# Modulation weights split over the layer: eight blocks first, forty as pairs of column tiles between other stages, and rope inside the projection

## The chip, the cores and the metric

The kernel runs on one core of a Trainium2 chip. The metric is the device time of one execution in microseconds (us), the median over several executions. The engines are named as in the profile: PE is TensorE (PEld its weight loads), DVE VectorE, ACT ScalarE, POOL GpSimd, SP SyncE, which here only issues the weight transfers. A name with q behind it is an engine's queue of instructions.

## The reference

Two layers work on 6 tiles of 128 tokens (4 latent, 2 context) with 1024 channels. What matters here, shortened:

```python
mod = silu(c) @ w_mod[l] + b_mod[l]        # (6 * 1024), one row for the latents, one for the context
sh1, sc1, g1, sh2, sc2, g2 = split(mod, 6)
h = layer_norm(x) * (1 + sc1) + sh1
p = h @ w_in[l]                            # 22 blocks of columns: conv, A, B, D, O
yA = windowed_gqa(rope(qA), rope(kA), vA)  # A: 4 + 2 tiles of 128 channels turned by rope
yB, yC, yD = neighbourhood(...), conv_module(...), mlstm(...)
y = merge(yA, yB, yC, yD, gates(h)) @ w_out[l]
x = layer_norm(alpha * x + g1 * y)         # deepnorm, first sub-layer
h2 = layer_norm(x) * (1 + sc2) + sh2
x = layer_norm(alpha * x + g2 * experts(h2, router(h2)))   # 16 experts, each takes its own tokens
```

w_mod of a layer is 1024 x 6144, i.e. 24 blocks of 256 columns (1 MB each). The shift and scale vectors are needed with channels on partitions (`modc`), the gates g1 and g2 as rows.

## The kernel before

All work goes through 27 stages. At the end of each, the four engines PE, ACT, DVE and POOL meet: `Stages.leave` (L472) drains the engine, adds one to a semaphore and waits until all four have done so. A drain on POOL also waits for the transfers that POOL issued. The stages of layer 0 are: modulation, modulate (transpose the normalised tiles, scale and shift), in-projection of the conv, A and B blocks, rope, attention, in-projection of the D blocks, mLSTM, O projection, merge, out-projection, router, gather, experts, closing norm. The closing norm of layer 0 shares its time with layer 1's modulation. Layer 1 has the same stages, shorter ones since it needs no context output.

SP runs ahead of the stages. It loads 1 MB blocks of weights into a ring of four slots (`raw`, `load`), in one fixed order: 24 of w_mod, 22 of w_in, 24 of gate and branch, 4 of w_out, then the experts'. A slot is free when PE has used it (`ring_used`) or, for the w_in and gate blocks, when its remainder is split off. Of those blocks ACT copies the high part (L457) and POOL or DVE computes the low part (L460) into `part`, two blocks deep. For the conv, A and B blocks DVE does that between the taps of the depthwise convolution (31 taps over 4 tiles, given out evenly between blocks); for the others, and for the first two blocks of a stage, POOL does it. PE takes a block only when its remainder is there.

The modulation stage: PE multiplies the 1024 x 2 columns `s2T` with each block into two PSUM rows; DVE adds the bias over two blocks at a time (L1445) into `mod_row`; 32 small transposes (L762) and four DVE instructions (L1451) make `modc`; POOL stores `mod_row` to `mod_d` in DRAM (L577), from which the gate rows are read later (L635).

```python
for c in range(MOD_BLOCKS):                          # PE, L753
    w = take()
    passes(psf[0:2, ...], [(s2T[:, k, :], w[:, k, :]) for k in range(KD)]).then_inc(ring_used, 1)
```

Rope is a stage of its own behind the in-projection: six matmuls (L815) with a rotation matrix, three DVE instructions each. Behind POOL's last remainder of the in-projection POOL stores the convolution's input to the attention, `yc_d` (L592). In the out-projection PE waits for the router's weights before the first tile, though it needs them from the third on. At the start of the experts DVE sets three buffers to zero (L1919), POOL one (L656), and then DVE computes the first two remainders (L1868).

## Time and profile before

| | us |
|---|---|
| median of 3 runs | 4023.34 |
| lowest, highest | 4022.8, 4026.16 |
| the profiled execution | 4029.46 |
| its span in the trace | 4027.8 |
| TensorE busy | 3587.6 (89%) |
| VectorE busy | 2335.1 (58%) |
| ScalarE busy | 1588.6 (39%) |
| GpSimd busy | 741.7 (18%) |

The span is the time from the first to the last instruction of the profiled execution. Busy shares are averages over stages that differ much, so that they say little of any one stage. The stages' ends in the trace are the moments at which the engines leave a meeting; for layer 0: 107.9, 138.0, 391.0, 404.9, 597.8, 716.9, 787.9, 834.4, 1270.1, 1398.2, 1431.8, 1471.2, 2179.3 and 2283.8.

### The profile page before, as it was taken

Reading aid. Unit: us, or ns where it says so; the run is one execution under the profiler, and the core shown is the slowest. Engines: PE = TensorE matmul, PEld = TensorE weight load, DVE = VectorE, ACT = ScalarE, POOL = GpSimd, SP = SyncE. Lnnn points to the kernel's source line nnn. Section 1 sums busy time; section 2 is a strip of 40 time slices with the busy share of each in tenths; the row PEclk is TensorE's granted clock in tenths of the full one; section 3 lists DMA queues with packets and bytes.
Section 4 is the critical chain, followed back from the end, with each engine's and each line's share of the span. In section 5 each row is a group of like instructions: output and inputs, shape, how many; then the busy total and the mean of one; then the engine's idle time right before and its main releaser. Section 6 shows DMA issues by size and latency. Waiting matters only on the chain. (4 is left out here: it accounts for less than half of the span.)

```text
span 4027.8 us, 49164 instructions
## 1 busy us (share of the span) xinstructions
PE 3587.6 (89%) x18834; PEld 2743.3 (68%) x18834; DVE 2335.1 (58%) x3474; ACT 1588.6 (39%) x2055; POOL 741.7 (18%) x403
## 2 busy tenths in 40 slices
PE   8797889899998869999998699798899868999994
PEld 3697569888887756666664388578766655666663
DVE  2295761511111659999897464751322258999996
ACT  0321762511110236666662222553311126666662
POOL 0100012111110013332231100011222103233221
PEclk9899999899999889999998799899999979999997
DMA  9121022011112228888887621131122217999994
GB/s 317 61 73 69 21 79 71 12 68 56 40 63 74 94 82 306 311 309 311 308 307 273 206 79 63 43 100 53 37 94 94 84 64 270 327 325 334 331 324 152
DMA packets 329455, 632.73 MB, mean 157 GB/s; under 512 B 12288, under 2 KB 102480, under 8 KB 322880
## 3 DMA queue, kind: packets, MB, share of 16 engines
q1 hardware_dynamic: 309056, 557.88, 40.0%
q0 software_dynamic: 20240, 72.64, 5.3%
q8 instruction: 111, 1.82, 0.2%
q14 instruction: 48, 0.39, 0.0%
HBM read 613.95 MB, written 16.52 MB: 157 GB/s over the span
## 5 line engine op out<-in xcount | busy, mean ns | idle before, releaser
L733 PE MATMUL ps<-hx,part 128*128 128x384 f32 (+2 forms) x4704 | 928.9, 357 | 32.2 <-DVEq L474 17.3
L733 PEld LDWEIGHTS ps<-hx,part 128*128 128x128 f32 x4704 | 834.4, 190 | 115.7 <-DVEq L474 18.5
L1094 PE MATMUL ps<-part,hx 128*96 128x512 f32 x3072 | 759.0, 397 | 38.3 <-DVE part L1868 31.1
L1094 PEld LDWEIGHTS ps<-part,hx 128*96 128x96 f32 x3072 | 492.7, 163 | 249.1 <-DVE part L1868 49.7
L1868 DVE TENSOR_TENSOR part<-raw,part 128x2048 fp32r<-128x2048 f32 x256 | 615.4, 2404 | 26.1 <-ACT part L1356 24.3
L1356 ACT ACTIVATE part<-raw 128x2048 fp32r<-128x2048 f32 x256 | 489.9, 1914 | 214.0 <-PE ps L1094 188.9
L460 POOL TENSOR_TENSOR part<-raw,part 128x2048 fp32r<-128x2048 f32 x52 | 237.6, 4570 | 1165.9 <-ACT part L457 1165.9
L1094 PE MATMUL ps<-hx 128*96 128x512 f32 x1536 | 378.9, 395 | 4.0 <-DVE hx L1868 2.4
L1094 PEld LDWEIGHTS ps<-hx 128*96 128x96 f32 x1536 | 247.3, 162 | 112.9 <-POOL hx L680 5.7
L733 PE MATMUL ps<-part,hx 128*128 128x256 f32 (+2 forms) x2208 | 307.5, 301 | 15.5 <-DVEq L474 15.5
L733 PEld LDWEIGHTS ps<-part,hx 128*128 128x128 f32 x2208 | 289.0, 194 | 30.9 <-DVEq L474 16.2
L1761 DVE TENSOR_TENSOR area<-ps,area 128x768 f32<-128x768 f32 (+1 forms) x48 | 39.6, 825 | 425.6 <-PE ps L733 425.6
L733 PE MATMUL ps<-area,raw 128*128 128x384 f32 (+1 forms) x768 | 285.3, 521 | 0.0
L1875 DVE TENSOR_TENSOR area<-area,ps 128x512 f32<-128x512 f32 x340 | 225.6, 679 | 73.2 <-PE ps L733 73.2
L1868 DVE TENSOR_TENSOR hx<-raw,hx 128x2048 fp32r<-128x2048 f32 x96 | 233.8, 2436 | 49.2 <-ACT hx L1356 49.2
L1356 ACT ACTIVATE hx<-raw 128x2048 fp32r<-128x2048 f32 x128 | 244.5, 1910 | 43.1 <-PE ps L1094 32.3
L733 PE MATMUL ps<-hx 96*128 96x512 f32 x680 | 214.1, 414 | 47.0 <-DVE hx L1913 38.9
L733 PEld LDWEIGHTS ps<-area,raw 128*128 128x128 f32 x768 | 145.0, 190 | 107.9 <-issue 46.0
L680 POOL TENSOR_TENSOR hx<-raw,hx 128x2048 fp32r<-128x2048 f32 x32 | 148.1, 4628 | 350.0 <-ACT hx L1356 350.0
L1489 DVE SCALAR_TENSOR_TENSOR area<-area,conv_c 128x512 f32<-128x512 f32 x360 | 208.8, 659 | 0.0
L733 PEld LDWEIGHTS ps<-hx 96*128 96x128 f32 x680 | 126.0, 194 | 106.2 <-issue 49.4
L733 PE MATMUL ps<-raw,s2T 128*2 128x256 f32 x768 | 174.6, 391 | 24.5 <-DVE area L1445 10.0
(244 smaller groups left out, 3807.8 us busy)
## 6 DMA issues: line engine op xcount, KB each, us to landing
raw<-in_w_exp_gate SPq DMA_DIRECT2D x128, 1024.0 KB, 5.3
raw<-in_w_exp_up SPq DMA_DIRECT2D x128, 1024.0 KB, 5.3
raw<-in_w_exp_down SPq DMA_DIRECT2D x128, 1024.0 KB, 5.4
raw<-in_w_mod SPq DMA_DIRECT2D x48, 1024.0 KB, 6.4
raw<-in_w_in SPq DMA_DIRECT2D x44, 1024.0 KB, 4.8
raw<-in_w_gate SPq DMA_DIRECT2D x32, 1024.0 KB, 5.4
area<-in_bias POOLq DMA_DIRECT2D x32, 512.0 KB, 4.0
raw<-in_w_branch SPq DMA_DIRECT2D x16, 1024.0 KB, 8.6
```

The source lines that it names most:

```text
L460: self.tt.tensor_tensor(part[:, q % 2, 1, :], raw[:, n % RING, :], part[:, q % 2, 0, :].bitcast(f32), ALU.subtract).then_inc(S("split_p"), 1)
L680: nc.gpsimd.tensor_tensor(expert_part(s, 1), raw[:, (r0 + s) % RING, :].rearrange("p (k n) -> p k n", k=4), expert_part(s, 0).bitcast(f32) ...
L733: last = mm(dst, a, b, start=i == 0, stop=i == len(pairs) - 1)
L1094: last = mm(ps[0:CAP, bank, :], x, y, start=kh == 0 and a == 0, stop=kh == 1 and a == len(pairs) - 1)
L1356: fn(expert_part(s, 0), src, ACT.Copy).then_inc(S("split_h"), 1)
L1489: own(V.scalar_tensor_tensor(y, x, conv_c[:, j, tap:tap + 1], y, ALU.mult, ALU.add))
L1761: V.tensor_tensor(even(t_) if ctx_out else t_[:, 0:LAT], p_, s_, ALU.mult).then_inc(*S("z_part", l).by(1))
L1868: V.tensor_tensor(expert_part(s, 1), src, expert_part(s, 0).bitcast(f32), ALU.subtract).then_inc(S("split_v"), 1)
L1875: V.tensor_tensor(a, a, ps[:, scatter_bank(c, ncomb), :], ALU.add).then_inc(*S("e_acc", l).by(1))
```

## The change

Only the eight blocks with sh1 and sc1 of layer 0 stay in front. The other 40 (16 of layer 0, 24 of layer 1) are taken in 20 pairs by `mod_pair(g, i)` of PE. A pair computes 4 x 128 columns as four column tiles, one in each quarter of the PSUM partitions (rows 0, 32, 64, 96), one k at a time through all four. `MOD_GROUPS` gives the six groups of pairs and their places, all in layer 0: two pairs between the transposes of modulate (group 0), four ahead of A and B blocks (1), four ahead of D blocks (2), one between the halves of the O projection and one at its end (3), eight in the router stage (4 and 5), of which two stand ahead of the wait for the affinities and six ahead of the slots' transposes. DVE's `move_mod(g)` adds the bias in four instructions of two partitions; POOL's `load_mod_bias(g)` and `store_mod(g)` issue four small transfers for each run of pairs of one layer. `modc` of sh2 and sc2, and all four of layer 1, are read back from `mod_d` by POOL's `load_modc`, eight numbers for each partition, each number apart. SP follows `PLAN`.

Further parts: rope's matmuls stand inside the A and B blocks (`ROPE_AT`), with one PSUM bank and one temporary; DVE does the turns of the first three between remainders and of the others at the end; the copies out of PSUM have three groups of banks instead of four (D blocks: two instead of three); the taps are given out over 7 blocks instead of 8; one meeting is gone from each layer. POOL's store of `yc_d` stands ahead of its last two remainders. ACT's first two high parts of layer 0 stand behind tiles 3 and 4 of modulate, and in the O projection both next ones at the end. PE waits for `router_in` at the third tile. DVE's first two expert remainders stand ahead of the zeroing, and POOL's zeroing in the router stage.

TensorE from the program's start: the modulation and modulate stages, and the start of the in-projection. Before:

```order
L733 MATMUL ps<-raw,s2T 2x256 x192
L762 MATMUL ps<-consts,area 128x2 x32
L771 MATMUL ps<-consts,area 128x128 x48
L733 MATMUL ps<-hx,part 128x512 x24
L733 MATMUL ps<-hx,part 128x256 x24
```

Now:

```order
L835 MATMUL ps<-raw,s2T 2x256 x64
L875 MATMUL ps<-consts,area 128x2 x16
L884 MATMUL ps<-consts,area 128x128 x8
L862 MATMUL ps<-raw,s2T 2x128 x32
L884 MATMUL ps<-consts,area 128x128 x8
L862 MATMUL ps<-raw,s2T 2x128 x32
L884 MATMUL ps<-consts,area 128x128 x32
L835 MATMUL ps<-hx,part 128x512 x24
```

A block in front is 8 matmuls of 256 columns; 64 of 192 are left, and each `L862 ... x32` is one pair.

TensorE in the A and B blocks of the in-projection of layer 0 and behind them. Before (the last row is rope):

```order
L733 MATMUL ps<-hx,part 128x384 x288
L733 MATMUL ps<-part,hx 128x144 x144
L733 MATMUL ps<-hx,part 128x384 x384
L733 MATMUL ps<-part,hx 128x256 x288
L815 MATMUL ps<-area 128x512 x6
```

Now, from the second block on (L931 is rope):

```order
L862 MATMUL ps<-raw,s2T 2x128 x32
L835 MATMUL ps<-part,hx 128x144 x144
L931 MATMUL ps<-area 128x512
L862 MATMUL ps<-raw,s2T 2x128 x32
L835 MATMUL ps<-hx,part 128x384 x144
L931 MATMUL ps<-area 128x512
L835 MATMUL ps<-hx,part 128x384 x96
L931 MATMUL ps<-area 128x512
L835 MATMUL ps<-hx,part 128x384 x96
L931 MATMUL ps<-area 128x512
L835 MATMUL ps<-hx,part 128x384 x48
L835 MATMUL ps<-part,hx 128x256 x120
```

Two of the four pairs and four of the six rope matmuls are seen; each stands in the one queue of TensorE ahead of the rest of the projection.

GpSimd from the D blocks of layer 0 (stores of attention's buffers) to the end of the O projection. Before:

```order
L612 DMA area<-yc_d 128x3072
L613 DMA ya_d<-area 128x3072
L460 TENSOR_TENSOR part<-raw,part 128x2048 x6
L622 TENSOR_TENSOR area<-area 128x512 x12
L460 TENSOR_TENSOR part<-raw,part 128x2048 x2
L629 DMA area<-ya_d 128x3072
```

Now:

```order
L697 DMA area<-yc_d 128x3072
L698 DMA ya_d<-area 128x3072
L620 DMA area<-in_b_mod 2x2x128 x8
L512 TENSOR_TENSOR part<-raw,part 128x2048 x6
L638 DMA modc<-mod_d 128x8x1 x4
L643 TENSOR_SCALAR modc<-modc 128x16
L628 DMA mod_d<-area 2x2x128 x8
L713 TENSOR_TENSOR area<-area 128x512 x12
L620 DMA area<-in_b_mod 2x2x128 x4
L512 TENSOR_TENSOR part<-raw,part 128x2048 x2
L628 DMA mod_d<-area 2x2x128 x4
L724 DMA area<-ya_d 128x3072
```

The bias loads stand ahead of the six remainders, the `modc` loads and eight stores behind them; the same kind of stores stands behind the remainders of the O projection.

The diff, cut to its core:

```diff
+MOD_FIRST = 8
+MOD_GROUPS = (((0, 4), (0, 5)), ((0, 6), (0, 7), (0, 8), (0, 9)), ((0, 10), (0, 11), (1, 0), (1, 1)),
+              ((1, 2), (1, 3)), ((1, 4), (1, 5), (1, 6), (1, 7)), ((1, 8), (1, 9), (1, 10), (1, 11)))
+MOD_BANKS = (4, 7, 4, 4, 7, 5)
+ROPE_AT = (12, 15, 17, 19, 25, 28)
+MOD_AB, MOD_D, MOD_O = (5, 6, 7, 8), (15, 16, 17, 18), (21,)
...
@@ GpSimd
-                for p in range(2, MOD_BLOCKS // BIAS):
-                    pool.wait_ge(*S("mod_row", l).at((p - 1) * BIAS // 2))
-                    load_mod_bias(p)
-                pool.wait_ge(*S("mod_row", l).at(MOD_BLOCKS // 2))
-                load(mod_d[l], mod_row[0:2, :]).then_inc(*S("mod_out", l).by(16))
-                pool.wait_ge(*S("mod_out", l).at(16))
+                def store_mod(g):
+                    pool.wait_ge(*S("mod_moved", 0).at(g + 1))
+                    for layer, p, i, n in mod_runs(g):
+                        dst = mod_d[layer, :, 4 * P * p:4 * P * (p + n)].rearrange("s (q c n) -> c s q n", q=n, c=4)
+                        for c in range(4):
+                            load(dst[c], mod_tiles(g)[32 * c:32 * c + 2, 0, i * P:(i + n) * P].rearrange("s (q n) -> s q n", q=n)
+                                 ).then_inc(*S("mod_stored", 0).by(16))
+                def load_modc(layer, vs):
+                    for v in vs:
+                        row = (0, 1, 3, 4)[v]
+                        for s in range(2):
+                            load(modc[:, v, :, s], mod_d[layer, s, row * D:(row + 1) * D].rearrange("(k p) -> p k", p=P),
+                                 allow_slow_non_contiguous=True).then_inc(*S("modc_in", l).by(16))
+                    pool.wait_ge(*S("modc_in", l).at(32 * len(vs)))
...
                 split.mixers_to(l, 2)
+                if l == 0:
+                    load_mod_bias(0)
+                    store_mod(0)
+                    load_mod_bias(1)
+                    stored(0)
                 st.leave()
...
                 pool.wait_ge(*S("conv_tapped", l).at(1))
+                load(yc_d[:, :, 0:full * P], yc[:, :, 0:full * P]).then_inc(*S("yc_out", l).by(16))
                 split.mixers_from(l, S_D)
                 split.mixers_to(l, S_D + 2)
-                load(yc_d[:, :, 0:full * P], yc[:, :, 0:full * P]).then_inc(*S("yc_out", l).by(16))
-                st.leave()
...
                 split.mixers_to(l, S_O + 2)
+                if l == 0:
+                    load_modc(0, (2, 3))
+                    store_mod(2)
+                    stored(2)
...
@@ TensorE
+                def mod_pair(g, i):
+
+                    if g and i == 0:
+                        pe.wait_ge(*S("mod_moved", 0).at(min(g, 4)))
+                    ws = [take(), take()]
                     for k in range(KD):
+                        for c in range(4):
+                            last = mm(ps[32 * c:32 * c + 2, MOD_BANKS[g], i * P:(i + 1) * P], s2T[:, k, :],
+                                      ws[c // 2][:, k, c % 2 * P:(c % 2 + 1) * P], start=k == 0, stop=k == KD - 1)
+                            if k == KD - 1 and c % 2:
+                                last.then_inc(ring_used, 1)
...
+                def rope(j):
+                    if j == 0:
+                        pe.wait_ge(*S("rope_in", l).at(32))
+                        pe.wait_ge(*S("ab_out", l).at(6))
+                    if j >= 1:
+                        pe.wait_ge(*S("rope_done", l).at(j))
                     src = y_v[0][:, j, 0:LAT] if j < FB else kA[:, j - FB, 0:LAT]
-                    mm(ps[:, j % 2, :], rot, src, start=True, stop=True).then_inc(*S("rope_rot", l).by(1))
+                    mm(ps[:, 6, :], rot, src, start=True, stop=True).then_inc(*S("rope_rot", l).by(1))
...
-                pe.wait_ge(*S("router_in", l).at(16))
                 for t in range(full + 2):
...
+                        if t == 2:
+                            pe.wait_ge(*S("router_in", l).at(16))
...
+                if l == 0:
+                    mod_pair(4, 0)
+                    mod_pair(4, 1)
                 pe.wait_ge(*S("r_aff", l).at(1))
...
@@ VectorE
-                share = -(-len(taps) // (S_D - S_AB - 2))
-                for q in range(S_AB + 2, S_D):
+                share = -(-len(taps) // (S_D - S_AB - 3))
+                for q in range(S_AB + 2, S_D - 1):
                     convolve(share)
                     split.mixers_to(l, q + 1)
+                    if q == S_AB + 6:
+                        if l == 0:
+                            move_mod(1)
+                        dve.wait_ge(*S("rope_in", l).at(32))
+                    if q >= S_AB + 6:
+                        rope(q - S_AB - 6)
...
+                for s in range(AHEAD):
+                    if not rest_rank(s)[0]:
+                        rest(0, s)
                 for v, cols in ((put, TOK), (y_hi, D), (y_lo, D)):
```

## Rows read from the trace of the kernel before

**Rows 1.** The page's part 4: the chain that ended last, by engine.
```profile
PE 25%; DVE 4%; issue 4%; ACT 2%; DMA 1%; POOL 1%; POOLq 0%; DVEq 0%; ACTq 0%; SPq 0%
```

**Rows 2.** Windows, one for each of these stages; the header names the columns.
```profile
core 0: us, PE busy (x) PEld busy (x) DVE busy (x) ACT busy (x) POOL busy (x), PEclk, DMA share, GB/s
0.00:107.90 107.90, 89.10 (x416) 35.19 (x416) 23.68 (x52) 4.00 (x9) 9.31 (x21) 0.97 0.93 308
107.90:138.00 30.10, 11.00 (x48) 9.00 (x48) 11.40 (x6) 26.91 (x56) 11.86 (x3) 0.56 0.20 70
138.00:391.00 253.00, 236.20 (x1488) 227.79 (x1488) 160.71 (x268) 48.16 (x61) 10.76 (x5) 0.97 0.19 67
...
597.80:716.90 119.10, 111.69 (x704) 107.24 (x704) 14.77 (x29) 33.82 (x40) 28.63 (x8) 0.98 0.22 71
...
787.90:834.40 46.50, 39.09 (x312) 38.42 (x312) 12.31 (x24) 9.49 (x15) 9.10 (x2) 0.94 0.07 24
...
1398.20:1431.80 33.60, 2.26 (x12) 1.38 (x12) 28.17 (x59) 1.57 (x2) 1.00 (x2) 0.50 0.02 3
1431.80:1471.20 39.40, 38.50 (x160) 31.40 (x160) 0.00 (x0) 18.68 (x24) 0.00 (x0) 0.95 0.00 0
...
2179.30:2283.80 104.50, 90.27 (x416) 35.93 (x416) 67.92 (x112) 3.72 (x13) 7.49 (x14) 0.91 0.82 274
...
2526.60:2540.50 13.90, 8.46 (x12) 2.86 (x12) 11.43 (x18) 0.00 (x0) 0.00 (x0) 0.75 0.00 1
```

**Rows 3.** Timeline of VectorE: start, duration, engine, line, operation (idle before).
```profile
45.26 0.68 DVE L1445 TENSOR_TENSOR area<-ps,area 2x512 f32<-2x512 f32 x1 [6.23 <-PE ps L733]
```

**Rows 4.** Timeline of VectorE: layer 1's last standardise.
```profile
2245.34 0.81 DVE L1431 TENSOR_SCALAR area<-area,stat 128x1024 f32<-128x1024 f32 x1
```

**Rows 5.** Groups by form of the whole run: remainders on GpSimd, DMA issues.
```profile
L460 POOL TENSOR_TENSOR part<-raw,part 128x2048 fp32r<-128x2048 f32 x52 | 237.6, 4570 | 1165.9 <-ACT part L457 1165.9
...
L561 POOL DMA_DIRECT2D area<-in_b_mod x6 | 3.1, 519 | 52.9 <-DVE area L1445 46.4 <-DMA x_d<-area 6.5
```

**Rows 6.** Timeline, all engines, at the start of the out-projection, layer 0.
```profile
1268.07 0.37 SPq L510 DMA_DIRECT2D raw<-in_w_out  x1
...
1272.56 0.90 POOL L636 DMA_DIRECT2D area<-in_w_router  x1
...
1283.39 18.90 PE L733 MATMUL ps<-raw,area 128*128 128x256 f32 x73 [15.35 <-DMA area<-in_w_router]
```

**Rows 7.** DMA issues of the whole run: count, KB each, median us to landing.
```profile
raw<-in_w_mod SPq DMA_DIRECT2D x48, 1024.0 KB, 6.4
raw<-in_w_in SPq DMA_DIRECT2D x44, 1024.0 KB, 4.8
...
area<-in_w_router POOLq DMA_DIRECT2D x2, 64.0 KB, 9.7
```

**Rows 8.** The same place in layer 1, TensorE.
```profile
3185.76 17.46 PE L733 MATMUL ps<-raw,area 128*128 128x256 f32 x69 [12.83 <-DMA area<-in_w_router]
```

**Rows 9.** Groups by form of the whole run (busy us, mean ns): modulation matmuls.
```profile
L733 PE MATMUL ps<-raw,s2T 128*2 128x256 f32 x768 | 174.6, 391 | 24.5 <-DVE area L1445 10.0 <-ACT s2T L1125 8.8 <-DMA raw<-in_w_mod 4.7
```

**Rows 10.** Timeline of TensorE in the attention stage, layer 0.
```profile
439.01 1.14 PE L832 MATMUL ps<-area 128*64 128x128 f32 x16 [0.34 <-ACT area L1212]
```

**Rows 11.** Groups by form of the whole run: the rope's matmuls.
```profile
L815 PE MATMUL ps<-area 128*128 128x512 f32 x24 | 16.6, 824 | 35.7 <-ACTq L474 32.6 <-DVE area L1518 3.0
```

**Rows 12.** Timeline of VectorE in the in-projection, layer 0.
```profile
329.05 2.29 DVE L460 TENSOR_TENSOR part<-raw,part 128x2048 fp32r<-128x2048 f32 x1
331.25 14.24 DVE L1489 SCALAR_TENSOR_TENSOR area<-area,conv_c 128x256 f32<-128x256 f32 x27
```

**Rows 13.** Timeline of GpSimd at the end of the in-projection, layer 0.
```profile
380.99 0.56 POOL L592 DMA_DIRECT2D yc_d<-area  x1
```

**Rows 14.** Timeline of VectorE at the end of the router stage, layer 0.
```profile
1425.64 6.11 DVE L1849 TENSOR_TENSOR part<-iotas,area 128x512 fp32r<-128x512 f32 x10
```

**Rows 15.** Timeline of VectorE at the start of the experts, layer 0.
```profile
1471.22 9.09 DVE L1919 TENSOR_SCALAR hx<-consts 96x768 fp32r<-96x768 f32 x3 [39.47 <-ACTq L474]
```

**Rows 16.** Timeline of TensorE at the start of the experts, layer 0.
```profile
1483.55 4.69 PE L1094 MATMUL ps<-part,hx 128*96 128x512 f32 x12 [13.22 <-DVE part L1868]
```

More of the change, by code:

```diff
@@ L968, in _ @@
                 for half in range(2):
+                    if l == 0 and half:
+                        mod_pair(3, 0)
                     w = take_split()
@@ L1034, in _ @@
                 last.then_inc(*S("r_affT", l).by(1))
+                if l == 0:
+                    mod_pair(4, 2)
+                    mod_pair(4, 3)
+                    for i in range(4):
+                        mod_pair(5, i)
                 pe.wait_ge(*S("slots", l).at(1))
@@ L1174, in copies @@
                             between[g]()
-                        act.wait_ge(*pa.of(B_IN + b, j))
+                        if l == 0 and what == "vB" and idx == (0, 0):
+                            act.wait_ge(*S("mod_stored", 0).at(128))
+                        act.wait_ge(*pa.of(ORD[l]["in", b], j))
                         bank = 2 * (g % depth)
@@ L1292, in _ @@
                     fn(sig_o[:, g % 2, :], ps[:, g % 2, 0:QC], ACT.Sigmoid).then_inc(*S("o_sig", l).by(1))
-                    if t == full - 1:
+                    if t == full - 1 and (l or half):
                         split.mixers_to(l, S_O + half + 3)
@@ L1521, in _ @@
                     dve.wait_ge(*S("rope_done", l).at(j + 1))
-                    V.tensor_tensor(q, q, rope_s[:, j % 2, :], ALU.add)
+                    own(V.tensor_tensor(q, q, rope_s, ALU.add))
+                share = -(-len(taps) // (S_D - S_AB - 3))
+                for q in range(S_AB + 2, S_D - 1):
+                    convolve(share)
+                    split.mixers_to(l, q + 1)
+                    if q == S_AB + 6:
+                        if l == 0:
+                            move_mod(1)
+                        dve.wait_ge(*S("rope_in", l).at(32))
+                    if q >= S_AB + 6:
+                        rope(q - S_AB - 6)
+                assert not taps
+                own.wait()
+                dve.drain().then_inc(*S("conv_tapped", l).by(1))
+                split.mixers_to(l, S_D)
+                for j in range(S_D - S_AB - 7, 6):
+                    rope(j)
                 st.leave()
@@ L1926, in _ @@
                 dve.drain().then_inc(*S("e_yL", l).by(2))
-                for s in range(AHEAD):
-                    if not rest_rank(s)[0]:
-                        rest(0, s)
                 with turns(dve, E // 2 - 1) as i:
```

318 lines of the change are left out of this document (202 added, 116 removed).

## The prediction, made before the changed kernel ran

> **What bounds the kernel now.** I read the chain that ended last first. TensorE holds 25% of the span there, VectorE and issue 4% each, all other engines 2% or less [rows 1]: no single engine is the limit everywhere, and the rest of the span is many short hand-overs. So the change has to be priced stage by stage, and the second view is the windows [rows 2], cut where the four engines meet. In a window the reader is to see which engine is nearly full and whether DMA is. Four kinds appear:
> - 0.00 to 107.90 (modulation, layer 0) and 2179.30 to 2283.80 (closing norm of layer 0 with layer 1's modulation): DMA share 0.93 and 0.82 at 308 and 274 GB/s. Each is 24 blocks of 1 MB with two output rows, and weight delivery is the limit.
> - 138.00 to 391.00, 597.80 to 716.90, 787.90 to 834.40: TensorE busy 236 of 253, 112 of 119, 39 of 46.5, DMA share 0.07 to 0.22. There is room for weights, none for TensorE time.
> - 1398.20 to 1431.80 (router): VectorE busy 28 of 33.6, TensorE 2.3, DMA share 0.02.
> - 1431.80 to 1471.20 (gather): TensorE 38.5 of 39.4, DMA 0.00.
>
> The kernel before spends about 3.4 us per block (1.05 MB at 308 GB/s) on 48 modulation blocks with nothing beside them, while DMA idles elsewhere.
>
> **What the change removes**, in us.
> 1. Modulation stage of layer 0. Eight blocks stay. VectorE's fourth addition, which ends block 8, is at 45.26 and takes 0.68 [rows 3]; 16 transposes, two additions and the meeting add 2: the stage ends at 48.0 where it ended at 107.9. **-59.9**.
> 2. Layer 1's modulation. Its last block loads are gone; what is left is VectorE's last standardise at 2245.34 + 0.81 [rows 4]. Beside it GpSimd loads four parameters and then eight `modc` loads. VectorE is no longer last; GpSimd is. Layer 0's last stores, four issues (0.52 each [rows 5]) and their landing reach to about 2240, an estimate; eight issues of 0.90 (nearest row: `w_router`, also 1024 pieces, [rows 6]) give 2247, and 2.5 for landing 2249.5, where the stage ended at 2283.8. **-34.3**. Both ends for the landing: 0.5 and 9.7 [rows 7].
> 3. The rope as a stage of its own: 13.9 in layer 1 [rows 2] and the same in layer 0. See 5 and 10.
> 4. `router_in` waited on at the third tile only. TensorE idles 15.35 until 1283.39 for `w_router` [rows 6]. The last of four w_out blocks is issued at 1268.07; with 4.8 to land, as for w_in [rows 7], TensorE can start at 1272.9. **-10.5**. Layer 1: 12.83 of idle until 3185.76 [rows 8]; by the same landing **-8.0**. VectorE needs rows that GpSimd issues just ahead of `w_router`, but not before TensorE's first run, which is 18.90 long [rows 6], so they are there.
>
> **What it adds.** First a pair's price, which no row shows. One block now is 16 records in 174.6 / 48 = 3.64, so 0.227 a record of 256 columns [rows 9]; a record of 128 columns is half, 0.114. A pair is 64 such records. One after another: 7.3. Four at once: 1.8. The nearest row has two column tiles: 16 records in 1.14 [rows 10], 0.071 each where 0.114 would be serial, a gain of 1.6 from two tiles, so that tiles do overlap. I take **2.1**, near the lower end. The Trainium skill (TensorE: Matmul & The Clock Gate, section "Why this matters for your kernels") gives 2.38 for three column tiles; by that share a pair would be 2.3 and the sum 2 us more, an estimate.
>
> 5. In-projection of layer 0. Four pairs (+8.4), six rope matmuls on TensorE (0.824 each [rows 11], +4.9), and depth 3 instead of 4. VectorE must convolve 31 taps per block instead of 27, from 14.24 to 16.3, plus its 2.29 remainder [rows 12]: 18.6 a block, where TensorE needs 16.6, so that it eats its lead of about one block by block 13, and `rope(1)` waits some 6 for VectorE. I put the stalls at 15. `yc_d` was issued at 380.99 [rows 13], behind GpSimd's last remainder (4.6 [rows 5]) and ScalarE's part and copy (2.3), so TensorE ended at 374.1; now at 374.1 + 8.4 + 4.9 + 15 = 402.4, and the last remainder 6.9 later: 409.3. The store held the meeting until 391.0; it is now issued ahead of the last two remainders and is covered. With the rope the two stages ended at 391.0 + 13.9 = 404.9. **+4.4**. Both ends: no stall gives -10.6, twice the stall +19.4.
> 6. Stage 1 (modulate, 30.1 long, [rows 2]). ScalarE's first two parts move behind tiles 3 and 4, so GpSimd's remainders (4.57) end near 30 instead of running beside. Then, in one queue: four bias DMAs (2.1), landing 3 to 5, VectorE's move 1.7, four stores 2.1, landing 2, four more bias issues 2.1. **+13**, to 43. The pairs sit in TensorE's idle time (11 busy of 30).
> 7. D projection: four pairs, +8.4. Behind the last remainder GpSimd has four `modc` loads (3.6 issue, 3 landing), 1, and eight stores (4.2) that must land (2.5). **+22.7**. The eight bias loads ahead are hidden under TensorE.
> 8. O projection: one pair ahead (2.1), two remainders at the end instead of one (+4.6), four stores (2.1), landing 2.2. **+11**.
> 9. Router of layer 0: 16 blocks, four of them already in the ring. The first of the other twelve lands 6.4 [rows 7] after a slot is free at about 1.2, eleven more follow at 3.4: 45.0. Then the pair's end 0.9, slot transposes 0.8, a copy 0.3 and VectorE's 6.11 [rows 14]: 53.1 against 33.6. **+19.5**. The store and second move of groups 4 and 5 lie under the gather's 39.4 (VectorE and DMA empty there), as do the first expert loads.
> 10. Layer 1's in-projection and rope: as in 5 without pairs. The meeting at 2526.6 stood behind a smaller store, its last remainder some 9 earlier at 2517.6; 5.6 for the rope matmuls and their waits: 2523.2 against 2540.5. **-17.3**.
> 11. Start of the experts, both layers. TensorE starts at 1483.55, 12.35 after the barrier, after VectorE's zeroing of 9.09 [rows 15] and its first remainder [rows 16]. Now the remainders come first, so TensorE may start 8 earlier, but the third remainder waits for the zeroing: **-4.5** each, -9.
>
> Sum: -59.9 -34.3 -18.5 +4.4 +13 +22.7 +11 +19.5 -17.3 -9 = **-68.4**. The terms come from the profiled execution of 4029.46 (span 4027.8, 1.7 around it); it is 6.1 above the median of 4023.34. Nothing in the terms scales with that, so I subtract from the median: 4023.3 - 68.4 = **3955**.
>
> **Rivals.**
> - *The filled places are not that expensive (larger gain).* My stalls in 5 (15), the landing chains in 6 and 7 (about 10 together) are estimates that can be zero: -25, **3930**. For: DMA share is 0.2 there. Against: the `yc_d` row, where a store held a meeting 10 us. 0.12.
> - *VectorE becomes the bound of the in-projection.* With 18.6 per block against 16.6 the lead may be gone at once, and blocks behind a pair arrive late in the ring of four: 8 us for two loads, at eight places 2 to 4 each, beside 15 for VectorE. +20 to +40, **3985**. For: [rows 12]. Against: TensorE's own rate hides single loads. 0.14.
> - *The four tiles run one after another.* A pair costs 7.3: 12 pairs ahead of the router at +5.2, 62, and eight in it, where 7.3 against 6.8 of delivery adds 4: +66, **4021**, no change. For: the two-tile row gains 1.6 and not 2. Against: it gains. 0.06. That the tiles are thus not what the diff says is this case.
> - *Single-element loads* (the other side). `load_modc` reads 1024 numbers of 4 bytes per DMA. I priced its issue 0.90 as for 1024 longer pieces. If each instead costs the 9.7 that `w_router` took to land, one behind the other, 12 of them cost 12 x (9.7 - 0.9) = 106: **4061**, slower. It decides from 68 / 12 = 5.7 extra each. For: the row of 9.7 is the only such load. Against: beside it, megabyte loads competed for the queues. The Trainium skill (DMA: Bandwidth & Descriptors, section "Rules for kernel authors") says that a non-contiguous last dimension becomes one descriptor per element and is to be rearranged; no row here shows what that costs. 0.05.
>
> **How the numbers follow.** Forecast 0.63, with its own range 3938 to 3975 (the both-ends of 5, and 2.1 against 1.8 and 3 for a pair). Low end 3925 takes in the larger gain; high end 3995 the VectorE case; the last two, 0.11, and a tail stay out. A measurement of this kernel tells about 0.2% (8 us) from no change. Faster by more: 0.63 + 0.12 + 0.14 + a part of the rest = 0.90; within: 0.05; slower: 0.05.
>
> **What the changed profile would show.** Fourth addition near 45, the first meeting at 48; 64 records of a pair within 1.8 to 2.5; the in-projection's end at 409 less 47 (59.9 gained, 13 lost); the router about 53 long with TensorE idle on `raw<-in_w_mod`; TensorE's wait ahead of the out-projection gone; GpSimd's DMA rows ahead of layer 1's first stage, 0.9 each. Wrong if a pair's rows add up to 7, if `modc` loads show more than 1.5 each, if VectorE rows ahead of TensorE's idle in the in-projection exceed 15 in all, or if the expert loads, which now start later, leave TensorE idle there.

## The result and the profile after

The changed kernel takes 3951.85 (3946.67 to 3958.99, 4 runs), against 4023.75 for the kernel before beside it: a ratio of 0.9822, 95% interval 0.9805 to 0.9839, 71.9 less. The profiled execution took 3951.19, its span is 3949.5.

The windows of the changed kernel, in the stages of [rows 2] (there is no window for rope: it is inside the third), and the in-projection of layer 1 as the last:

```profile
core 0: us, PE busy (x) PEld busy (x) DVE busy (x) ACT busy (x) POOL busy (x), PEclk, DMA share, GB/s
0.00:45.80 45.80, 32.34 (x144) 12.32 (x144) 18.01 (x42) 4.00 (x9) 7.79 (x18) 0.96 1.02 338
45.80:89.70 43.90, 12.75 (x176) 9.92 (x176) 10.10 (x11) 26.80 (x56) 18.37 (x15) 0.62 0.45 165
89.70:360.80 271.10, 258.48 (x1756) 242.65 (x1756) 175.46 (x290) 47.91 (x61) 13.02 (x9) 0.95 0.25 90
...
553.20:693.40 140.20, 119.97 (x960) 113.33 (x960) 17.44 (x33) 33.81 (x40) 41.27 (x29) 0.94 0.38 129
763.50:819.70 56.20, 41.46 (x440) 40.32 (x440) 10.77 (x28) 9.49 (x15) 13.27 (x10) 0.89 0.41 132
1373.50:1428.20 54.70, 23.56 (x524) 16.50 (x524) 28.17 (x59) 1.57 (x2) 8.44 (x7) 0.72 0.83 269
...
2167.80:2237.30 69.50, 0.00 (x0) 0.00 (x0) 60.05 (x96) 3.72 (x13) 13.90 (x20) 0.50 0.15 47
...
2267.40:2474.90 207.50, 196.12 (x1116) 176.08 (x1116) 122.44 (x158) 45.32 (x57) 10.97 (x5) 0.99 0.21 74
```

The reader is to see that the first window and the closing norm (2167.80) lost 62 and 35, and that the DMA share rose where it had been low: 0.07 to 0.41 in the O projection, 0.02 to 0.83 in the router. TensorE's busy time grew by 22 in the in-projection (rope's matmuls, which had a stage of their own, are in it), by 8 in the D projection, and by 21 in the router, where it fills idle time. All stages, from the meetings in the two traces, beside the terms of the prediction:

| stage | before | after | moved | predicted |
|---|---|---|---|---|
| modulation, layer 0 | 107.9 | 45.8 | -62.1 | -59.9 |
| modulate | 30.1 | 43.9 | +13.8 | +13 |
| in-projection and rope | 266.9 | 271.1 | +4.2 | +4.4 |
| D projection | 119.1 | 140.1 | +21.0 | +22.7 |
| O projection | 46.5 | 56.3 | +9.8 | +11 |
| out-projection, both layers | 220.6 | 203.6 | -17.0 | -18.5 |
| router, layer 0 | 33.6 | 54.8 | +21.2 | +19.5 |
| closing norm, layer 0 | 104.6 | 69.5 | -35.1 | -34.3 |
| in-projection and rope, layer 1 | 226.6 | 207.6 | -19.0 | -17.3 |
| experts, both layers | 1371.8 | 1357.4 | -14.4 | -9 |
| all others | | | -0.7 | 0 |
| **span** | 4027.8 | 3949.5 | -78.3 | -68.4 |

The two profiled executions differ by more than the medians (78.3 against 71.9): that of before was 5.7 above its median, that of the changed kernel 0.7 below.

Now the lines that answer to single rows. A pair on TensorE, its 64 records in one row of the timeline, in modulate, in the in-projection and in the router:

```profile
47.78 2.59 PE L862 MATMUL ps<-raw,s2T 128*2 128x128 f32 x64
...
239.72 2.20 PE L862 MATMUL ps<-raw,s2T 128*2 128x128 f32 x64
...
1387.01 3.59 PE L862 MATMUL ps<-raw,s2T 128*2 128x128 f32 x64 [7.28 <-DMA raw<-in_w_mod]
...
1405.88 1.93 PE L862 MATMUL ps<-raw,s2T 128*2 128x128 f32 x64 [2.19 <-DMA raw<-in_w_mod]
```

A pair costs 1.93 where the granted clock is 1.00, 2.20 and 2.59 in stretches at 0.86 and 0.72, and 3.59 at 0.50; over all twenty the mean is 2.32. In this trace of the router the pairs behind idle waits of 7.28, 4.78 and 5.77 run at the lower level, those behind 2.19 and 2.17 at the full one.

The in-projection has stretches at 0.50 too, in its middle, where the kernel before had none. Two rows of TensorE with the same 72 matmuls, and the window of the stretch:

```profile
214.44 8.26 PE L835 MATMUL ps<-part,hx 128*128 128x144 f32 x72
224.40 13.59 PE L835 MATMUL ps<-part,hx 128*128 128x144 f32 x72 [1.70 <-ACT area L1318]
...
226.70:240.30 13.60, 13.60 (x68) 11.92 (x71) 13.60 (x28) 2.85 (x7) 0.00 (x0) 0.50 0.00 0
```

TensorE had waited 1.70 for ScalarE's copy out of PSUM, which stands in ScalarE's queue behind the high part (1.91) of a weight block; ScalarE had waited 8.70 for that block to land. Then the clock fell to 0.50 for 13.7, and once more for 3.4 behind the wait of 2.64 ahead of a rope matmul. GpSimd's queue at the end of the D projection, and around VectorE's move in modulate:

```profile
675.56 4.51 POOL L512 TENSOR_TENSOR part<-raw,part 128x2048 fp32r<-128x2048 f32 x1 [12.65 <-ACT part L509]
...
680.02 3.57 POOL L638 DMA_DIRECT2D modc<-mod_d  x4
...
685.93 4.42 POOL L628 DMA_DIRECT2D mod_d<-area  x8
...
75.61 2.24 POOL L620 DMA_DIRECT2D area<-in_b_mod  x4
...
81.61 1.72 DVE L1586 TENSOR_TENSOR area<-ps,area 2x256 f32<-2x256 f32 x4 [4.87 <-DMA area<-in_b_mod]
83.62 2.17 POOL L628 DMA_DIRECT2D mod_d<-area  x4 [5.78 <-DVE area L1586]
85.78 2.15 POOL L620 DMA_DIRECT2D area<-in_b_mod  x4
```

In the first, 680.07 is when the last remainder is done, and 13.3 pass until the meeting at 693.4: loads, their landing, one instruction, stores, their landing, one behind the other. In the second, 14.1 pass from 75.6 to 89.7 in the same way. TensorE at the start of the out-projection of layer 0 (compare [rows 6]: 15.35 of idle), and VectorE and TensorE at the start of the experts (compare [rows 15] and [rows 16]):

```profile
1258.84 30.58 PE L835 MATMUL ps<-raw,area 128*128 128x256 f32 x128 [5.48 <-DMA raw<-in_w_out]
...
1469.39 5.36 DVE L2035 TENSOR_TENSOR part<-raw,part 128x2048 fp32r<-128x2048 f32 x2 [29.00 <-ACT part L1493]
1474.68 1.75 DVE L2089 TENSOR_SCALAR hx<-consts 96x768 fp32r<-96x768 f32 x3
...
1472.61 4.55 PE L1228 MATMUL ps<-part,hx 128*96 128x512 f32 x12 [6.24 <-DVE part L2035]
```

The experts' first matmul comes 5.4 after the meeting instead of 12.35, which is 6.9 earlier. The three zeroings now take 1.75 in all. They took 9.09.

### The profile page after: what moved, and what is told of

It is laid out like the page before. It is cut to its first block, busy times and chain, and to the rows that moved or that the text cites. A ratio compares the mean times of both kernels' runs of the same rounds, so it can differ in the third digit from the quotient of the medians.

```text
span 3949.5 us, 50430 instructions
## 1 busy us (share of the span) xinstructions
PE 3482.3 (88%) x19426; PEld 2718.0 (69%) x19426; DVE 2316.6 (59%) x3472; ACT 1588.2 (40%) x2055; POOL 779.9 (20%) x467
## 4 chain that ended last, share of the span: by engine, by line
PE 65%; DVE 11%; issue 9%; ACT 6%; DMA 5%; POOL 2%; POOLq 1%; DVEq 0%; PEld 0%; ACTq 0%; PEldq 0%; SPq 0%
PE ps L835 42%; PE ps L1228 13%; ACT hx L1493 2%; PE ps L953 2%; DVE part L2035 2%; PE ps L985 2%; DMA raw<-in_w_exp_down 1%; DMA raw<-in_w_mod 1%; DMA raw<-in_w_exp_gate 1%; PE ps L971 1%; DVE area L1638 1%; ACT area L1349 1%; POOL hx L782 1%; POOLq L526 1%; PE ps L973 1%
## 5 line engine op out<-in xcount | busy, mean ns | idle before, releaser
L835 PEld LDWEIGHTS ps<-hx,part 128*128 128x128 f32 x4704 | 834.0, 190 | 146.4 <-POOLq L526 46.4
L835 PE MATMUL ps<-part,hx 128*128 128x256 f32 (+2 forms) x2208 | 313.8, 304 | 17.3 <-DVEq L526 15.6
L835 PEld LDWEIGHTS ps<-area,raw 128*128 128x128 f32 x768 | 145.0, 190 | 107.9 <-issue 46.0
L1444 ACT ACTIVATE area<-ps,mgate_b 128x768 f32<-128x768 f32 x32 | 28.8, 901 | 388.6 <-PE ps L835 388.6
```

What stands on the lines that cost most here:

```text
L835: last = mm(dst, a, b, start=i == 0, stop=i == len(pairs) - 1)
```

## The experiments

Eight kernels leave one part of the change out or alter it, one is the changed kernel again, two go on from it. A stage's length is read from the meetings in each trace. A stage whose work is the same in two kernels differed by less than 2, but by up to 4 in the in-projection of layer 0, 3 in its mLSTM and O projection and 5 in the experts of each layer. In the in-projection the reason can be read: the stretch at 0.50 is 13.7 long in the changed kernel and 20.5 in the three kernels whose stage took 274.6 to 275.1 instead of 271.

**Do the four tiles run at once?**

```diff
-                    for k in range(KD):
-                        for c in range(4):
+                    for c in range(4):
+                        for k in range(KD):
```

> The changed kernel, with the loops of a pair swapped: all eight k of one column tile, then the next tile. Same matmuls, same results, but consecutive matmuls use the same tile. Theory (the four tiles of a pair run at once, and that is why a pair costs 2): a pair's 64 records take 7.3 instead of 1.9 to 2.2 at the full clock; the in-projection and the D projection of layer 0 grow by 21 each, modulate and O projection by about 10 each, the router stage by 4 (delivery 6.8 a pair against 7.3) if the granted clock there is high and by up to 60 if it stays at half: +66 to +120 on the changed kernel, so 4015 to 4070. Rival (tiles are served one after another anyway and the price of a pair is issue, not overlap): no stage moves by more than 1, total within 5 of 3952.

Measured: 3991.81, ratio 0.9919 (0.9903 to 0.9936), 40 above the changed kernel. TensorE in modulate, and the group of pair matmuls of the whole run in this kernel, then the same group in the changed one:

```profile
55.47 5.85 PE L862 MATMUL ps<-raw,s2T 128*2 128x128 f32 x64
...
L862 PE MATMUL ps<-raw,s2T 128*2 128x128 f32 x1280 | 119.6, 277 | 2.9 <-DMA raw<-in_w_mod 2.5 <-PEq L526 0.4
```

```profile
L862 PE MATMUL ps<-raw,s2T 128*2 128x128 f32 x1280 | 46.4, 307 | 24.8 <-DMA raw<-in_w_mod 24.4 <-PEq L526 0.4
```

A serial pair costs 5.85 at the full clock, all twenty 119.6 against 46.4. So the tiles do overlap: 3.0 times where the pair runs at the full clock in both kernels (5.85 against 1.93), 2.6 times over all. Modulate grew by 6.3, the in-projection by 9.1, the D projection by 15.6, O by 4.7, the router by 4.5, and mLSTM, whose work is the same, by 3.1. The direction was as expected, the size not: a serial record of 128 columns takes 0.091, not the half of 0.227 that I had taken (0.114), and the granted clock was higher (0.99 in the in-projection and 0.93 in the router, against 0.95 and 0.72 in the changed kernel). In the in-projection that gave part of it back: four pairs are 15.7 longer, the stage 9.1. There the wait of 1.70 for ScalarE's copy and both stretches at 0.50 are gone. In the router, where TensorE's busy time grew by 26 and the stage by 4.5, the pairs stand beside the delivery of weights.

**What do the modc loads cost?** Two kernels.

```diff
-    load(modc[:, v, :, s], mod_d[layer, s, row * D:(row + 1) * D].rearrange("(k p) -> p k", p=P),
+    load(modc[:, v, :, s], mod_d[layer, s, row * D:(row + 1) * D].rearrange("(p k) -> p k", p=P),
...
+    load(modc[:, v, :, :].rearrange("p k s -> p (k s)")[:, s * KD:(s + 1) * KD],
+         mod_d[layer, s, row * D:(row + 1) * D].rearrange("(p k) -> p k", p=P))
```

> The changed kernel, with the twelve modc loads reading eight neighbouring numbers for each partition (128 pieces of 32 bytes instead of 1024 of 4), so that the shift and scale vectors sit at wrong channels; no other work changes. Theory (an issue costs 0.9 to 1.0 because of the 1024 pieces, and the landing 2.9): issue falls to about 0.55, landing to 2; the D projection's end is 2.5 earlier, the closing norm's end 2.5 earlier where VectorE's 2234.8 then ends it: -5 in all. Rival (single elements are what costs, as the slower case of the prediction had it): several us per load go, -20 or more.

> The changed kernel, with the twelve modc loads reading and writing eight neighbouring numbers for each partition: 128 pieces of 32 bytes on both sides, so that the shift and scale vectors sit at wrong places. (The earlier variant left the destination at every second number, so its pieces stayed single numbers.) Theory A (the piece count costs): issue falls from 0.97 to about 0.55 as for the small bias loads, landing from 2.9 to 2; D projection -3, closing norm -2.5. Theory B (an issue's price lies elsewhere and 1024 pieces are free): issue and landing stay, no stage moves.

The first (first + line) moved nothing (3954.45; issue 0.968 in place of 0.970), which says only that it was a poor test: its destination still took every second number, so that the pieces stayed single. The second (last two lines) has them together on both sides. The group of these issues in it, and in the changed kernel:

```profile
L638 POOL DMA_DIRECT2D modc<-mod_d x12 | 7.1, 598 | 2.0 <-DMA mgate_b<-in_b_gate 2.0
```

```profile
L638 POOL DMA_DIRECT2D modc<-mod_d x12 | 11.6, 970 | 2.0 <-DMA mgate_b<-in_b_gate 2.0
```

An issue costs 0.37 more with single numbers, and a landing 2.9 against 1.9. The D projection was 2.1 and the closing norm 2.5 shorter, near the -3 and -2.5 expected; the median, 3950.75, cannot tell 4.6. A solid destination with a scattered source was not run. The slower rival needed 5.7 extra for each load: the runs show 0.37 for each issue and 1.0 for a landing that several share.

**What made the experts start earlier?** The first of two kernels puts VectorE's remainders behind the zeroings again, the second GpSimd's memset of the accumulator back to the start of the experts.

```diff
-                for s in range(AHEAD):                      # e3: behind the drains again
-                    if not rest_rank(s)[0]:
-                        rest(0, s)
...
-                nc.gpsimd.memset(acc, 0.0).then_inc(*S("acc_zero", l).by(1))    # e4: from the router to the experts' start
```

> The changed kernel, with VectorE's first two expert remainders again behind the three zeroings; GpSimd's zeroing of the accumulator stays in the router stage. Theory A (the gain of 7 in each expert stage is the order, as predicted): TensorE's first expert matmul comes 9 later, both expert stages +5 to +7. Theory B (VectorE's zeroing was slow only because GpSimd's memset ran beside it: 9.09 before, 1.75 after): the zeroings stay at about 1.8, TensorE starts 1.8 later, stages +2 at most.

> The changed kernel, with GpSimd's zeroing of the accumulator again at the start of the experts; VectorE's remainders stay first. Theory A (order decides): no change in TensorE's start, since GpSimd's memset of 5.2 is not waited for by the first matmuls apart from the copies behind it on GpSimd (3.2): +3 at most. Theory B (the two engines hinder each other): VectorE's first remainder of 2.3 is stretched to about 5 or more beside the memset, and TensorE starts 5 to 7 later.

3958.53 (ratio 0.9837, 0.9817 to 0.9856) and 3957.98 (0.9835, 0.9816 to 0.9855). Timelines of the start of the experts: the first kernel, then the second.

```profile
1471.45 4.00 DVE L2086 TENSOR_SCALAR hx<-consts 96x768 fp32r<-96x768 f32 x3 [26.59 <-ACTq L526]
...
1475.87 4.49 DVE L2035 TENSOR_TENSOR part<-raw,part 128x2048 fp32r<-128x2048 f32 x2 [0.42 <-DVE hx L2086]
...
1478.22 0.82 PEld L1228 LDWEIGHTS ps<-part,hx 128*96 128x96 f32 x3 [8.08 <-DVE part L2035]
```

```profile
1469.65 5.22 POOL L758 MEMSET area<- 128x6144 f32 x1 [25.30 <-ACTq L526]
...
1471.76 4.50 DVE L2035 TENSOR_TENSOR part<-raw,part 128x2048 fp32r<-128x2048 f32 x2 [29.85 <-ACT part L1493]
...
1476.17 3.99 DVE L2089 TENSOR_SCALAR hx<-consts 96x768 fp32r<-96x768 f32 x3
...
1479.15 4.62 PE L1228 MATMUL ps<-part,hx 128*96 128x512 f32 x12 [10.41 <-POOL hx L769]
```

With the zeroings first but no memset beside them, TensorE starts 6.8 after the meeting, 1.4 later than in the changed kernel. With the memset at the start but the remainders first, 9.5 after it. Neither order alone brings back the 12.35 of before. The medians rose by 6.7 and 6.1, the expert stages of both layers together only by 1.8 and 3.6, less than such stages differ anyway, so that the medians don't price these orders; the rows below show what they do. What VectorE and GpSimd do at the same moment, in the kernel before, in the first of the two kernels and in the changed one:

```profile
1471.22 5.65 DVE L1919 TENSOR_SCALAR hx<-consts 96x768 fp32r<-96x768 f32 x1 [39.47 <-ACTq L474]
1471.24 5.22 POOL L656 MEMSET area<- 128x6144 f32 x1 [45.20 <-ACTq L474]
```

```profile
1471.77 0.92 POOL L767 CAST hx<-area 128x768 fp32r x1 [24.47 <-ACTq L526]
1472.88 2.03 POOL L769 TENSOR_TENSOR hx<-area,hx 128x768 fp32r<-128x768 f32 x1 [0.19 <-issue]
```

```profile
1468.59 1.81 POOL L769 TENSOR_TENSOR hx<-area,hx 128x768 fp32r<-128x768 f32 x1 [0.19 <-issue]
1469.39 3.16 DVE L2035 TENSOR_TENSOR part<-raw,part 128x2048 fp32r<-128x2048 f32 x1 [29.00 <-ACT part L1493]
```

The first zeroing (96x768) took 5.65 beside the memset, and 0.54 in the changed kernel, where GpSimd is idle. The other two (96x1024) took 1.30 and 2.29 before, beside GpSimd's copy and subtraction (L665, L667), and 0.68 each in the changed kernel. So of the 7.3 that the zeroings lost, 5.1 are the memset's and 2.2 the copy's and the subtraction's. That is why they take 4.00, and not 1.8 as theory B had it, in the first of the two kernels: the memset is gone, but the copy and the subtraction stand beside them. The remainders (4.50 for two) are not slowed by the memset, so theory B's stretched remainder was wrong; one is slowed by the subtraction, 3.16 instead of 2.28. What TensorE waits for in the second kernel is GpSimd's own copy and subtraction behind the memset. The Trainium skill (SBUF — State Buffer, section "Who interferes with whom") has it that VectorE and GpSimd share a pair of ports, that VectorE's copies and tensor-scalar instructions can take both, and that then one of the two engines is blocked for the other's whole instruction. It adds (section "SBUF: two separate sides") that a VectorE instruction with two inputs contends only with a GpSimd instruction that reads. The rows agree: a memset (no input) beside a remainder (two inputs) costs nothing, beside a zeroing nearly its whole length, and GpSimd's subtraction, which reads, does slow a remainder.

**How much of the in-projection's term is rope, how much the store?** In the first kernel rope is a stage of its own again (with the changed kernel's single buffer), in the second the store of `yc_d` is behind the last two remainders again.

```diff
-                         **{ROPE_AT[j]: lambda j=j: rope(j) for j in range(6)}},
...
+                st.leave()
+                for j in range(6):          # first kernel, behind a meeting; VectorE the same
+                    rope(j)
...
-                load(yc_d[:, :, 0:full * P], yc[:, :, 0:full * P]).then_inc(*S("yc_out", l).by(16))
                 split.mixers_from(l, S_D)
                 split.mixers_to(l, S_D + 2)
+                load(yc_d[:, :, 0:full * P], yc[:, :, 0:full * P]).then_inc(*S("yc_out", l).by(16))   # second kernel
```

> The changed kernel, with rope again as a stage of its own behind the in-projection (six matmuls and their turns behind one more meeting in each layer); the taps stay at 31 a block, the store of yc_d stays ahead of the last two remainders. Theory (the rope inside the stream pays for itself only in part: of the 19 that layer 1 gained in this place about 10 come from the store and 9 or less from rope): in layer 0 the in-projection falls by 7.9 of rope matmuls and 3.4 of waits, and 14 for rope comes back: +3 to +4 a layer, +7 in all. Rival (rope in the stream hides nearly all of its 13.9, as its place behind busy engines suggests): +12 or more a layer, +25 in all.

> The changed kernel, with GpSimd's store of yc_d again behind its last two remainders. Theory (this order alone holds the meeting for the landing of the store, 9.9 and 8.9 before): layer 0's in-projection +8 to +10, layer 1's +5 to +9, total +15. Rival (the landing overlapped something else, the gain was the rope): +3 at most in all.

3972.4 (0.9879, 0.9861 to 0.9896) and 3967.67 (0.9865, 0.9847 to 0.9882). Windows of the first kernel, in-projection of layer 0, its rope, and in-projection of layer 1 (whose rope stage is 18.6 long as well); then the second, both in-projections:

```profile
88.50:348.90 260.40, 251.01 (x1744) 239.75 (x1744) 163.72 (x272) 47.88 (x61) 13.03 (x9) 0.96 0.27 94
348.90:367.50 18.60, 12.45 (x12) 3.01 (x12) 11.89 (x18) 0.00 (x0) 0.00 (x0) 0.50 0.00 0
2273.30:2475.40 202.10, 190.64 (x1104) 173.83 (x1104) 110.84 (x140) 45.30 (x57) 10.99 (x5) 0.98 0.23 76
```

```profile
88.70:364.90 276.20, 258.29 (x1756) 242.46 (x1756) 175.37 (x290) 47.86 (x61) 12.98 (x9) 0.94 0.25 89
2277.50:2497.20 219.70, 199.68 (x1116) 178.99 (x1116) 122.53 (x158) 45.28 (x57) 10.92 (x5) 0.94 0.22 75
```

Rope apart costs 7.9 in layer 0 (260.4 + 18.6 against 271.1), between the two theories, and 13.1 in layer 1 (220.7 against 207.6), as the rival had it. The stage itself took 18.6, not 13.9, at a granted clock of 0.50: with one buffer each matmul waits for VectorE's first addition and then takes 2.08, where it took 1.0 to 1.1 at the full clock. With the 13.9 of [rows 2], which had two buffers, rope apart would cost 3.2 and 8.4, worked out and not run.

The in-projections of the second kernel are 5.1 and 12.2 longer, 17 in all where 15 was expected, but not all of the 12.2 is the store's. GpSimd's last remainder in layer 1, before, in the changed kernel and in this one:

```profile
2513.11 4.49 POOL L460 TENSOR_TENSOR part<-raw,part 128x2048 fp32r<-128x2048 f32 x1 [12.56 <-ACT part L457]
...
2470.11 4.49 POOL L512 TENSOR_TENSOR part<-raw,part 128x2048 fp32r<-128x2048 f32 x1 [13.46 <-ACT part L509]
...
2483.66 4.49 POOL L512 TENSOR_TENSOR part<-raw,part 128x2048 fp32r<-128x2048 f32 x1 [13.44 <-ACT part L509]
```

From its end to the meeting it is 9.0 before (2526.6), 0.3 in the changed kernel (2474.9) and 9.1 here (2497.2): the store costs 8.7 in layer 1, and in layer 0, by the same rows, 5.3. The other 3.5 of layer 1 are TensorE's, whose same matmuls took 199.7 instead of 196.1. So the 19.0 that layer 1 gained can be added up from the two traces: 8.7 from the store's place, 13.9 from the rope stage that is gone, less 3.5 by which TensorE, with rope's matmuls in between, now ends later behind the meeting (200.4 against 196.9). That leaves 10.4 for rope, 2 more than the 8.4 above, for in the kernel with rope apart TensorE ended 195.0 behind the meeting.

**The wait for the router's weights.**

```diff
+                pe.wait_ge(*S("router_in", l).at(16))
                 for t in range(full + 2):
...
-                        if t == 2:
-                            pe.wait_ge(*S("router_in", l).at(16))
```

> The changed kernel, with TensorE waiting for the router's weights ahead of the first tile of the out-projection again. Theory (10.1 and 6.9 of gain at this place are this wait): layer 0's out-projection back from 118.0 to about 128, layer 1's from 85.6 to about 92.5, nothing else moves. Rival (the first tile would have to wait for its w_out block or its rows nearly as long): under +3 each.

3965.75 (0.986, 0.9839 to 0.9881); the out-projections 125.6 and 92.9 against 118.0 and 85.6: +7.6 and +7.3, as the theory said, in layer 0 by 2.5 less. The median is 13.9 above the changed kernel's.

**What do the chains behind the last remainder cost, and the router's late blocks?** These go on from the changed kernel, which ran beside them as `c_after`.

> The changed kernel itself, as the measure beside the two versions that follow, on their chip: 3952, between 3945 and 3960.

It took 3951.95 (0.9825, 0.981 to 0.984).

```diff
+                if l == 0:
+                    load_mod_bias(0)                 # in the modulation stage
...
                 nc.gpsimd.memset(cpad, 0.0).then_inc(*S("conv_zero", l).by(1))
+                if l == 0:
+                    store_mod(0)                     # VectorE moves behind tile u == 1
                 split.mixers_to(l, 2)
...
-                split.mixers_to(l, S_O + 2)
-                if l == 0:
-                    load_modc(0, (2, 3))
-                    store_mod(2)
+                split.mixers_to(l, S_O + 1)
+                if l == 0:
+                    store_mod(2)
+                split.mixers_to(l, S_O + 2)
...
+                    store_mod(3)                     # in the merge, behind the load of ya_d
+                    stored(3)
+                    load_modc(0, (2, 3))
```

> The changed kernel with GpSimd's small transfers moved off the meetings of layer 0. The bias of the first group is loaded in the modulation stage, VectorE moves that group after the second tile, GpSimd stores it ahead of its remainders, and the next bias load stands at the start of the in-projection. In the D projection the stores stand between the last two remainders and the modc loads go to the merge; the stores of the O projection go to the merge as well. Theory (the chains behind the last remainders, 14, 13 and 4 long, are all that these stages lost): modulate 43.9 to about 31, D projection 140.1 to about 129, O projection 56.3 to about 52, -28 in all, 3924. Rival (the pairs themselves or the remainders' new places set the ends): each stage keeps at least half of what it lost, -14 or less.

3921.33, ratio 0.9751 (0.9736 to 0.9766), 30.6 below `c_after`. Windows of modulate, D and O projection:

```profile
45.40:76.00 30.60, 13.50 (x176) 10.69 (x176) 10.01 (x10) 26.89 (x56) 14.03 (x7) 0.64 0.54 204
543.60:673.70 130.10, 119.95 (x960) 113.31 (x960) 17.44 (x33) 33.79 (x40) 37.44 (x24) 0.98 0.40 138
743.80:794.60 50.80, 41.45 (x440) 40.32 (x440) 10.76 (x28) 9.49 (x15) 11.15 (x6) 0.93 0.37 120
```

They are 30.6, 130.1 and 50.8 long, against 42.8, 140.2 and 56.8 in `c_after`: -28, as expected. TensorE does the same work in them as in the changed kernel (119.95 of busy time in the D projection, 119.97 there), so the 28 are the chains'. They are not all that these stages paid: against the kernel before, the D projection is still 11 longer and the O projection 4, of which TensorE's busy time, with the pairs, is 8.3 and 2.4. Modulate is within 0.5 of its old length.

```diff
-    plan = [...] + pair(0, 0) + pair(0, 1) if l == 0 else []
+    plan = [...] + pair(0, 0) + pair(0, 1) if l == 0 else [("mod", layer, 2 * p + b) for layer, p in MOD_GROUPS[5] for b in range(2)]
...
+                else:                                # TensorE, layer 1's first stage
+                    for i in range(4):
+                        mod_pair(5, i)
```

> The version before this one, and the last four pairs (eight blocks of layer 1) taken in the closing norm of layer 0, where TensorE and the DMA queues are idle, instead of in the router stage; their store and the last modc load follow in layer 1. Theory (the router stage is as long as the delivery of its twelve late blocks): the router stage falls from 54.8 to 34 to 36, the closing norm stays within 2 of 69.5 since its end hangs on VectorE (67, plus 2.8 for the move) and no longer on GpSimd, gather and experts do not change: -18 to -20 on v1, 3905. Rival (late expert loads or the clock after an idle router stage take part of it back): -8 or less.

3907.61 (3901.68 to 3909.33, 5 runs), ratio 0.9711 (0.9697 to 0.9724). Windows of the router and the closing norm:

```profile
1346.50:1382.70 36.20, 14.81 (x268) 10.03 (x268) 28.17 (x59) 1.56 (x2) 8.45 (x7) 0.64 0.69 236
2123.80:2193.50 69.70, 11.97 (x256) 8.17 (x256) 62.71 (x100) 3.73 (x14) 13.61 (x21) 0.57 0.50 168
```

The router is 36.3 long between its meetings, 20.1 less than in the version before (56.4, as in `c_after`), and the closing norm 69.7 with four pairs in it. Of the 20 the median shows 13.7, less than the 18 to 20 expected. The spans differ by 13.0: the experts of layer 0 took 4.2 longer, mLSTM 3.3 and modulate of layer 1 2.2, while the in-projection of layer 0 took 4.0 less. Modulate of layer 1 has the new stores in it. For mLSTM the rows name the reason, first in the version before, then in this one:

```profile
673.70:743.80 70.10, 60.18 (x499) 58.61 (x499) 47.71 (x155) 39.46 (x138) 15.22 (x12) 0.92 0.01 1
```

```profile
669.30:742.60 73.30, 63.80 (x499) 62.13 (x499) 47.80 (x155) 39.46 (x138) 15.21 (x12) 0.86 0.00 1
```

TensorE's same 499 matmuls took 63.8 at a granted clock of 0.86 and 60.2 at 0.92, and in the in-projection its busy time differs in the same way, by 3.7 of the 4.0 (261.9 at 0.94, 258.2 at 0.95). Why the clock fell for longer in one kernel than in the other, no run here tells. In the experts, at 0.98 against 0.99, TensorE's busy time accounts for 2.2 of the 4.2. This version is the fastest: 44 below the changed kernel, 115 below the one before.

## Why the prediction was right

The forecast was 3955, the time is 3952, and each term has its sign and is within 3 of its size but for the experts. That the total came out within 3 is in part luck. The terms are worked out from a trace, and between the two traces the change is 78.3, 10 more than their sum; the medians show 6.4 less, since the two profiled executions lie 5.7 above and 0.7 below theirs. The largest misses are -5.4 in the experts, -2.2 in the modulation, and -1.7 each in the D projection and in layer 1's in-projection.

- **Modulation and closing norm** (-59.9, -34.3; measured -62.1, -35.1). Read straight from the row of the fourth addition and of the last standardise. The fourth addition came at 43.63, 1.6 earlier than in the row of before; the cause stays open. The loads of `modc` cost 0.97 each to issue, priced 0.90, and GpSimd ends the closing norm 2.5 behind VectorE, forecast 3.4.
- **The pair** (2.1). 1.93 at the full clock, 2.32 on the mean of all. The two-tile row was the right neighbour. That its price is the overlap is shown by the serial kernel; the rival with serial tiles had 7.3 for a pair where 5.85 is right, and 66 for the whole where 40 was measured.
- **In-projection, layer 0** (+4.4; measured +4.2). The sum hit, its parts less so. TensorE ended 263.7 behind the meeting, where it had been 236.3: 27.4 later, forecast 28.3. But the stalls, taken as 15, are 5: of the 271.1, TensorE is busy 258.5 and 7.4 lie behind its end. The ropes are 7.9 of busy time, not 4.9, and 6.4 more is the same matmuls, slower in the two stretches at 0.50. The prediction had no term for the clock; it came in by way of the stalls, and the terms' errors cancelled. VectorE did not become the bound: TensorE waits 3.4 for it ahead of rope's matmuls, and the other 1.7 for ScalarE's copy.
- **The chains on GpSimd** (+13, +22.7, +11; measured +13.8, +21.0, +9.8). Shown by the first of the two versions, which takes 28 of the 45 back without touching a pair.
- **Router** (+19.5; measured +21.2): delivery of twelve late blocks. TensorE's pairs there wait for `raw<-in_w_mod` 24.4 in all, and moving eight blocks away takes 20.1 off the stage.
- **Out-projection** (-18.5; measured -17.0), shown by the kernel that puts the wait back, for 14.9 of it.
- **Layer 1's in-projection** (-17.3; measured -19.0). The store is 8.7, booked 9. Rope is the part that was undersized: 13.9 gone, 3.5 come back, where 5.6 was booked.
- **Experts** (-9; measured -14.4). The step that failed is "the third remainder waits for the zeroing", which was to give back 3.5 of a start that is 8 earlier. The remainder does wait, but for a zeroing of 1.75 and not of 9.09: 5.1 of the 9.09 were the memset on GpSimd, which the change moved away, and 2.2 GpSimd's copy and subtraction, which are over by then. TensorE starts 6.9 earlier, the two expert stages are 7.5 and 6.9 shorter, and next to nothing is given back.

The slower rival was off by its size: single-number loads cost 0.4 to 1 extra, not 5.7.

## What to carry to other kernels

Work that is bound by the delivery of weights can be put into stages bound by a computing engine, where it costs TensorE's time for it (here about 2 a pair, against 6.8 for its two blocks in front) and whatever its small transfers cost at the end of a stage. Of the 45 that modulate, the D and the O projection grew by, 28 were loads and stores in line behind the last remainder, before a meeting, and only 11 TensorE's busy time. Put a store ahead of the last piece of long work on the same queue, so that its landing is covered, and look for a later stage with an idle engine and an idle queue before filling a short one. With column tiles, run through the tiles inside the k loop; here the other order cost three times as much.

## What the runs showed that was not expected

- A memset on GpSimd beside VectorE's zeroing stretches the latter from 0.54 to 5.65, but leaves a remainder (two inputs) at its 2.29; GpSimd's subtraction, which reads, does stretch one, to 3.16. Before costing a VectorE row, see what GpSimd does at that moment.
- A wait of 1.70 on TensorE, in the middle of a stage where it is otherwise busy, was followed by 13.7 at half the clock, in other kernels by 20.5. With serial pairs, which are longer, the wait and the stretch were gone, and part of the added work was returned.
- A DMA of 1024 single numbers costs 0.97 to issue and 2.9 to land, one of 128 pieces of 32 bytes, solid on both sides, 0.60 and 1.9. With a solid source alone nothing changed.
